# One layer's state recurrence over pairs of time steps: 128 scan steps in place of 256

## The reference

```python
lam_bar = jnp.exp(lam * dt)
b_bar = ((lam_bar - 1.0) / lam)[:, :, None] * b_mat
bu = jnp.einsum('gpc,bsgc->bsgp', b_bar, ug)
# states[t] = lam_bar * states[t-1] + bu[t], for t = 0 .. 255
_, states = lax.associative_scan(_linear_recurrence_combine, (decay, bu), axis=1)
y = jnp.einsum('gcp,bsgp->bsgc', c_mat, states).real
y = y + d_skip * ug
y = jax.nn.gelu(y)
return y * jax.nn.sigmoid(y @ w_glu + b_glu)
```

## Time and profile before

| what | us |
|---|---|
| three runs, median (lowest to highest) | 1106.88 (1104.37 to 1108.78) |
| the profiled execution: its own time | 1107.08 |
| its span in the trace | 1105.4 |
| TensorE busy | 1082.7 (98%) |
| VectorE busy | 617.5 (56%) |
| ScalarE busy | 402.2 (36%) |
| mean granted clock of TensorE | 0.994 of full |

### The profile page before, as it was taken

The page is one execution under the profiler, slowest core; times in us unless marked ns, Lnnn a source line. Parts: engine busy times, 40 slices in busy tenths (PEclk is TensorE's granted clock), DMA queues, the critical chain, the costliest instruction groups (busy, mean ns, idle before and its releaser), DMA issues.

```text
span 1105.4 us, 17516 instructions
## 1 busy us (share of the span) xinstructions
PE 1082.7 (98%) x7004; PEld 801.5 (73%) x7004; DVE 617.5 (56%) x1249; ACT 402.2 (36%) x652; POOL 6.0 (1%) x21
## 2 busy tenths in 40 slices
PE   9999999999999999999999999999999999999996
PEld 6988778998899999999799994444444444444442
DVE  4999997777568888887978762221111111111112
ACT  6522336466355554546676331111111111111112
POOL 2000000000000000000000000000000000000000
PEclk9999999999999999999999989999999999999998
DMA  8544323544245767776544598999999999999994
GB/s 301 172 161 145 102 89 114 172 172 134 76 153 174 231 231 242 240 255 193 186 138 131 215 405 371 426 429 427 427 426 428 428 427 428 427 427 427 427 427 165
DMA packets 44883, 302.62 MB, mean 274 GB/s; under 512 B 5248, under 2 KB 6400, under 8 KB 30976
## 3 DMA queue, kind: packets, MB, share of 16 engines
q1 hardware_dynamic: 41616, 287.59, 67.0%
q10 hardware_dynamic: 3184, 13.87, 3.5%
HBM read 300.39 MB, written 1.05 MB: 273 GB/s over the span
## 4 chain that ended last, share of the span: by engine, by line
PE 91%; DVE 4%; ACT 2%; issue 1%; DMA 1%; SPq 0%; ACTq 0%; DVEq 0%
PE psum L1989 90%; DMA ring<-in_stream 1%; DVE w_low L1143 1%; ACT w_high L653 1%; DVE arena L1143 1%; PE psum L2773 1%; DVE rt L1146 0%; PE psum L2779 0%; DVE x L1143 0%; DVE h L1146 0%; SPq L469 0%; SPq L472 0%; DVE h_low L1143 0%; DVE h_low L1146 0%; DVE arena L1140 0%
## 5 line engine op out<-in xcount | busy, mean ns | idle before, releaser
L1989 PE MATMUL psum<-experts_held,arena 128*64 128x512 f32 x1536 | 333.6, 593 | 2.2 <-DVE scatter_turned L1139 1.0
L1989 PEld LDWEIGHTS psum<-experts_held,arena 128*64 128x64 f32 x1536 | 111.2, 137 | 212.0 <-issue 211.1
L1143 DVE TENSOR_TENSOR w_low<-ring,w_high 128x1024 fp32r<-128x1024 f32 x150 | 180.4, 1219 | 35.7 <-ACT w_high L653 35.0
L653 ACT CAST w_high<-ring 128x1024 fp32r<-128x1024 f32 x150 | 154.5, 1047 | 63.1 <-DMA ring<-in_stream 54.9
L1989 PE MATMUL psum<-h_high,w_high 128*128 128x256 f32 x528 | 133.0, 287 | 3.9 <-ACT arena L736 1.8
L1989 PE MATMUL psum<-h_low,w_high 128*128 128x256 f32 x528 | 131.0, 283 | 0.0
L1989 PE MATMUL psum<-y_high,w_high 128*128 128x256 f32 x480 | 123.1, 285 | 0.5 <-issue 0.3
L1143 DVE TENSOR_TENSOR arena<-arena,psum 128x512 f32<-128x512 f32 (+1 forms) x31 | 19.3, 631 | 182.4 <-ACT arena L1072 181.6
L1989 PE MATMUL psum<-y_low,w_high 128*128 128x256 f32 x480 | 119.6, 283 | 0.0
L1989 PEld LDWEIGHTS psum<-h_high,w_high 128*128 128x128 f32 x528 | 101.2, 192 | 6.2 <-ACT arena L736 2.0
L1989 PEld LDWEIGHTS psum<-h_low,w_high 128*128 128x128 f32 x528 | 101.2, 192 | 0.2
(11 more groups left out here) (269 smaller groups left out, 1262.4 us busy)
## 6 DMA issues: line engine op xcount, KB each, us to landing
experts_held<-in_experts SPq DMA_DIRECT2D x84, 2048.0 KB, 27.2
ring<-in_stream SPq DMA_DIRECT2D x180, 512.0 KB, 3.5
experts_held<-in_experts ACTq DMA_DIRECT2D x12, 1024.0 KB, 7.3
experts_held<-in_experts SPq DMA_DIRECT2D x12, 1024.0 KB, 12.7
x<-in_xT SPq DMA_DIRECT2D x2, 512.0 KB, 7.7
out_y<-experts_held SPq DMA_DIRECT2D x4, 256.0 KB, 3.1
arena<-in_memT SPq DMA_DIRECT2D x1, 512.0 KB, 8.8
bbd<-in_ssm_b SPq DMA_DIRECT2D x1, 512.0 KB, 11.7
```

The costliest lines, as they stand in the source:

```text
L653: act.copy(wh[:, high_slot(m)], ring[:, n_ % RING]).then_inc(hi_ready, 1)
L1143: return dve.tensor_tensor(o, a, b, op)
L1989: return pe.matmul(o, a, b, start=start, stop=stop, skip_group_check=True)
```

## The change

The recurrence over single steps, s[t] = L s[t-1] + b[t], is run over pairs: s[2n+1] = L^2 s[2n-1] + (b[2n+1] + L b[2n]). The scan then has 128 steps.

- `uT` is stored with the even times first and the odd times behind (ScalarE's eviction of `u`). ScalarE makes a second copy `u_in` (8 copies on 32 partitions) in which each state tile has 64 rows, its channels at even and at odd times, with zeros in the rows of the neighbour tile. Two state tiles make a pair j of 0..7.
- The input weights are computed on VectorE (`b_both`: the matrix b, and b times `lam_bar`), transposed by TensorE (16 transposes, in two lots between the `v` units), and evicted by ScalarE (`b_in`, 4 copies). One input matmul then has 128 rows and 256 columns (two tiles of 128 pair steps).
- `recurrence(j)` runs 8 times in place of 16, each on the same 256 columns; it has four scans of 128 steps with the squared decay `rad2` in place of two of 256.
- Outputs at odd times come from the states with `cbd`, `neg`, as before, 128 columns. Outputs at even times t = 2n come from the state at 2n-1 with new matrices `cbd_even`, `neg_even` (the old ones times `lam_bar`; a second call of `output_matrices`), 127 columns, plus the direct part of the input at 2n: a block product `skip`, whose 32x32 blocks TensorE computes once (`skip_weights`, 32 matmuls of 32 columns) and ScalarE puts in place, and which is one 128x128 matmul in each `outputs_of`.
- The rotation table goes over 128 steps, so the last doubling goes away; its first power is the doubled angle.
- VectorE's order of the mixer is rewritten to two recurrences a round; the fillers stay as they are.
- The two halves of a wide expert place share one semaphore; `ssm_b` has 1 MB in place of 512 KB.

```diff
-        rot = view(0, 2, STILES, T)
+        rot = view(0, 2, STILES, STEPS)
+        rot_pairs = view(0, 2, SPAIRS, T)
...
+            for q in range(4):
+                for a in range(2):
+                    at = 64 * (q % 2) + 32 * a
+                    act.copy(u_in[at:at + 32, :, :, q // 2, q % 2],
+                             uT[32 * q:32 * q + 32, :, a * STEPS:a * STEPS + STEPS].rearrange(
+                                 "p (s i) n -> p s i n", s=2)).then_inc(u_ready, 1)
...
+            def turned_inputs(c):
+                act.wait_ge(b_turned, c + 1)
+                for half in range(2):
+                    act.copy(b_in[:, c, 4 * half:4 * half + 4].rearrange("p m n -> p (m n)"), psum[4 + half][:]
+                             ).then_inc(b_ready, 1)
...
+            link(tt_(rad2, rad, rad, ALU.mult))
+            tt_(ptmp[:, 0], fre, lr, ALU.mult)
+            tt_(ptmp[:, 1], fim, li, ALU.mult)
+            tt_(ptmp[:, 2], fre, li, ALU.mult)
+            link(tt_(ptmp[:, 3], fim, lr, ALU.mult))
+            tt_(gre, ptmp[:, 0], ptmp[:, 1], ALU.subtract)
+            link(tt_(gim, ptmp[:, 2], ptmp[:, 3], ALU.add))
 
             weights_low("q", 2)
-            link(dve.tensor_copy(powers[:, 0, 0], cos))
-            link(dve.tensor_copy(powers[:, 0, 1], sin))
+            dve.wait_ge(s_par, 16 * 2)
+            lrb, lib = (v.unsqueeze(2).to_broadcast([P, STILES, 32]) for v in (lr, li))
+            m1, m2 = (v[:, 0:STILES * 32].rearrange("p (j n) -> p j n", j=STILES) for v in (ta, tb))
+            tt_(m1, b_both[:, 0, :, 32:64], lrb, ALU.mult)
+            link(tt_(m2, b_both[:, 1, :, 32:64], lib, ALU.mult))
+            link(tt_(b_both[:, 0, :, 0:32], m1, m2, ALU.subtract))
+            tt_(m1, b_both[:, 0, :, 32:64], lib, ALU.mult)
+            link(tt_(m2, b_both[:, 1, :, 32:64], lrb, ALU.mult))
+            link(tt_(b_both[:, 1, :, 0:32], m1, m2, ALU.add))
+            dve.nop().then_inc(b_scaled, 1)
...
-            while w < T:
+            while w < STEPS:
...
                 for c in range(2):
-                    ins = dve.tensor_tensor_scan(wr[:, c], r_, vr[:, c], 0.0, ALU.mult, ALU.add)
+                    for b in range(2):
+                        some = slice(b * STEPS, b * STEPS + STEPS)
+                        ins = dve.tensor_tensor_scan(wr[:, c, some], rad2[:, 2 * j + b:2 * j + b + 1].to_broadcast([P, STEPS]),
+                                                     vr[:, c, some], 0.0, ALU.mult, ALU.add)
...
             recurrence(0)
+            masked_scores(0)
+            output_matrices(fre, fim, cbd, neg)
             recurrence(1)
-            masked_scores(0)
-            output_matrices()
-            recurrence(2)
-            recurrence(3)
             softplus(0)
+            output_matrices(gre, gim, cbd_even, neg_even)
             for r in range(1, ROUNDS):
-                recurrence(4 * r)
+                recurrence(2 * r)
                 log_weights(r - 1)
                 y_out(r - 1)
-                recurrence(4 * r + 1)
                 masked_scores(r)
-                recurrence(4 * r + 2)
-                if r == ROUNDS - 1:
-                    softplus(r)
-                recurrence(4 * r + 3)
-                if r < ROUNDS - 1:
-                    softplus(r)
+                recurrence(2 * r + 1)
+                softplus(r)
                 values_rest(r - 1)
...
+            split_rows(v_banks, "v", (h0h, h0l), 0, 1)
+            turned_inputs(0)
+            split_rows(v_banks, "v", (h0h, h0l), 1, 3)
+            turned_inputs(1)
+            split_rows(v_banks, "v", (h0h, h0l), 3, 4)
...
             def inputs_of(j):
 
-                i, q = j // 4, j % 4
-                for b in range(2):
-                    hbk.claim(pe, ("bu", j + b))
+                hbk.claim(pe, ("bu", j))
+                bank = hbk.bank(("bu", j))
+                moving = u_in[:, j // 4, j % 4 // 2, j % 2].rearrange("p b n -> p (b n)")
                 for c in range(2):
-                    for b in range(2):
-                        row = slice(32 * (q + b), 32 * (q + b) + 32)
-                        ins = mm(hbk.bank(("bu", j + b))[:, c * T:c * T + T], bbd[row, c, i], uT[row, i], True, True)
-                        if c:
-                            ins.then_inc(bu_done, 1)
+                    ins = mm(bank[:, c * T:c * T + T], b_in[:, c, j], moving, True, True)
+                ins.then_inc(bu_done, 1)
+
+            def skip_weights():
+
+                pe.wait_ge(ssm_ready, 2)
+                for j in range(STILES):
+                    i, q = j // 4, j % 4
+                    for c in range(2):
+                        ins = mm(STAT[32 * q:32 * q + 32, 32 * i:32 * i + 32], b_both[:, c, j, 32:64], cbd[:, c, j], c == 0,
+                                 c == 1)
+                ins.then_inc(skip_done, 1)
...
+                mm(STAT[:, 0:STEPS], skip[:, r], uT[:, r, 0:STEPS], True, False)
+                for even, terms in enumerate((((cbd[:, 0], 0), (neg, 3), (cbd[:, 1], 2), (cbd[:, 1], 1)),
+                                              ((cbd_even[:, 0], 0), (neg_even, 3), (cbd_even[:, 1], 2),
+                                               (cbd_even[:, 1], 1)))):
+                    for n, (matrix, product) in enumerate(terms):
+                        for q in range(4):
+                            made = st[:, (2 * r + q // 2) % 4, product, (q % 2) * STEPS:(q % 2) * STEPS + STEPS - even]
+                            o = STAT[32 * q:32 * q + 32, 1:STEPS] if even else STAT[32 * q:32 * q + 32, STEPS:T]
+                            ins = mm(o, matrix[:, 4 * r + q], made, False, n == 3)
```

151 lines of the change are left out of this document (97 added, 54 removed).

## The result

The changed kernel takes 1112.19 us (median of 6 runs, 1110.73 to 1112.83), the kernel before 1107.12 us in the runs beside it (6 runs, 1104.37 to 1108.78). The ratio is 1.0052, 95% interval 1.0039 to 1.0064: slower by about 5 us. The forecast was 1114.5 us with a range of 1110 to 1120.

The account below looks back on a forecast made before the run. TensorE was taken to set the mixer's pace, VectorE nearly full but just in time. Terms 3.4 + 2.0 + 2.6 + 0.9 - 1.3 = +7.6 us on 1107.08 gave 1114.7, 1114.5 for the median; range 1110 to 1120.

Parts of the forecast that it names:

- A: Weight units q3 and k2: VectorE's new work ahead of q3 makes TensorE stall, +3.4 us.
- B: The `v` units: 16 added transposes of 128x128 on TensorE, in two lots, +2.0 us.
- C: `skip_weights`: 32 matmuls, 64 records at 0.04 us each on TensorE, +2.6 us.
- D: Outputs, four rounds: narrower groups cost nothing extra, the new direct-part matmul adds +0.9 us.
- E: Inputs: full-height matmuls take 0.9 us a call in place of 1.06, eight times, -1.3 us.
- Rival 2: Skip weights and outputs: narrow instructions have a floor, +3.8 and +7 us or one of them; 1118.3 to 1125.3 us; chance 0.12.
- Rival 3: Stall at q3 and k2: smaller than forecast, 1 us or less; time 1112 us or less; chance 0.13.
- Rival 4: Mixer, 71.4 to 182.4 us: VectorE set the pace through unlisted waits; 1107 us or below; chance 0.10.
- Rival 1: Stall at q3: TensorE's idle 2.9 us halves the clock, costing 3.4 us more; time 1117.5 us; chance 0.15.
- Everything behind 190 us moves with TensorE: Behind the mixer: everything, expert weight DMA included, hangs on TensorE's progress, the stretch unchanged in length.

Follow-up runs that it names:

- e1: The changed kernel with VectorE's new work moved behind the weight units' low parts, transposes two units later, one filler before the first inputs; 1108.01 us, ratio 1.0014.
- e2: The kernel before with only VectorE's new work (seven small operations, six products, results unused) put ahead of q3's low part; 1108.93 us, ratio 1.0020.
- e6: The changed kernel with each input matmul reading only 64 of its 128 rows; 1112.42 us, ratio 1.0057 to the kernel before.
- e4: The kernel before with the eight odd-j recurrences leaving out their input products, sums and scans; 1106.68 us, ratio 1.0000.
- e8: The kernel before with six gate units done in two rounded parts, their low parts behind the rotation table's last doublings; 1115.96 us, ratio 1.0092.
- e9: The kernel before with six gate units in two parts, low parts at four places between operations of the last two table doublings; 1110.67 us, ratio 1.0035.
- e3: The kernel before with only the shared semaphore for the two halves of a wide expert place; 1106.43 us, ratio 1.0002.
- e11: The changed kernel with 150 empty instructions ahead of TensorE's program; 1112.68 us, ratio 1.0051 to the kernel before.
- e7: The changed kernel with VectorE's new work moved as in e1 and six gate units done in two rounded parts; 1104.63 us, ratio 0.9983.

## Why the prediction came out right

The mechanism held: TensorE set the pace, VectorE's savings were worth nothing, and its new work ahead of q3 stalled TensorE. By its terms, in us of TensorE's time in the mixer:

| term | predicted | measured | from |
|---|---|---|---|
| A, stall at q3 and k2 | +3.4 | +3.6 | 3.0 and 0.4 from start to start, 0.1 on the records behind each; e1 gives back 3.6, e2 puts 2.7 in |
| B, 16 transposes | +2.0 | +1.8 | two lots of 0.79 and 0.09 on the matmul behind each |
| C, `skip_weights` | +2.6 | +0.9 | 1.74 less 0.87 |
| D, outputs | +0.9 | +0.9 | four times 2.19 less 1.86, less 0.1 each that stood on the filler ahead before |
| E, inputs | -1.3 | -2.0 | about ten changes of shape fewer, 0.2 each |
| sum | +7.6 | +5.2 | mixer's length +5.15 |

The forecast for the time was right to 2.3 us, and the sum for the mixer to 2.4; the difference is two terms of size, C and E, both forecast too dear. That the times differ by the same 5.1 us as the mixers is partly luck: behind the mixer a wait of 1.1 us came in, and half clock at the router took some of it away (below). Term C failed at its price of 0.04 us a record, which was taken between a load of 32 columns (0.027) and the rows of one moving column (0.10): 64 records in 0.87 us are 0.014 each. Even the lower bound was too high, since it took a load's length for a distance between starts. These blocks stand on different rows and columns of the array, and their records, 0.2 us long each, overlap far more than that. Term E failed in that it counted only 0.16 for a call, and even its bound of -1.7 was passed: it priced the inputs by themselves, while a change of shape costs 0.1 us on the record at its other side as well, as e6 shows. Summed over the mixer, the inputs went from 8.48 to 7.43 us (0.10 of the second is left out here, the entry to `skip_weights`), the fillers from 92.04 to 90.77, of which 0.4 belong to D, and the last `v` unit lost 0.09.

Rival 2 (narrow instructions have a floor) is refuted on both halves: 0.014 us a record in `skip_weights` and not 0.10, and a group of four outputs takes half of what a wide one took. The Trainium skill ("TensorE: Matmul & The Clock Gate", section "Wait — 56ns, not 53.3ns?") says that starts are never less than about 25 ns apart, however small the matmuls. By that figure `skip_weights` would have taken 1.6 us, an estimate, where the trace has 0.87; the trace does not agree.

- *Rival 3* (the stall is 1 us or less) is refuted by the timeline: 3.6 us.
- *Rival 4* (VectorE set the pace) is refuted by e4, and by e1, where VectorE's gain stays and the loss is 1.5 us.
- *Rival 1* (the stall halves the clock) did not happen in the profile of the changed kernel (1.00 in [50.4, 53.8]), but did in e2's, where it cost 1.6 us, and at the longer stalls of e8 and e9. The clock falls in some executions and not in others, and the reason that was given against it is wrong: the wait of 1.8 us at 36.9 did not do it in the kernel before, but in four of the twelve profiles it did.
- *"Everything behind 190 us moves with TensorE"* held for 217 to 648 us and failed twice behind it. At the router, 6.8 us at half clock became 3.4, which took 1.7 us off the span; in all twelve profiles this stretch has 0, 3.4 or 6.8 us of it, whatever the kernel, and a profile pair is worth no more than that. At the last expert loads TensorE waits 1.1 us for a DMA, which gives some back.

That last wait is small but regular: 0.9 to 1.5 us in the changed kernel and the four made from it, 0 to 0.6 in the kernel before and the six made from it. In both the load stream runs at 427 GB/s through the whole stage, so the loads hardly lead. The last of the earlier trace rows and its like of after show the DMA share at 1.01 and 1.03. The times at which the 16 DMA engines report each of the last loads show the difference: against TensorE's progress the middle engine is as early in both to 0.3 us, and the slowest one is 1.5 to 1.8 us behind it in the kernel before and those made from it (2.4 in e9), and 2.5 to 2.9 in the changed one and those made from it. A load counts when the slowest has done its share. The shared semaphore doesn't put it back (e3). The code loads do, as far as the traces show: the lag moves in steps, and all 37 steps up of more than 0.25 us between one expert load and the next, in the twelve profiles from 700 us on, stand where a load of 16 KB of code starts (from 2.5 us before the first of the two landings to the second), though only 295 of the 940 pairs have one there. The last such step in the kernel before is from 0.6 to 1.5 us, with the code load of 1064.9; in the changed kernel it is from 1.4 to 2.5, with that of 1057.3. Why some programs end higher than others is open.

Also open is 1 us of bookkeeping: mixer +5.15 and the DMA wait +1.1 make more than the 5.1 us between the medians. The lowest times, 1110.73 and 1104.37 us, are 6.4 apart, which is about the two together, so the missing part is likely half clock, of which the median execution of the kernel before has more. One thing that goes this way is shown in e11: the clock was at 0.50 at 38 us there, TensorE came 1.7 us later to q3, and the stalls shrank to 1.7 us, so its mixer is as long as that of the changed kernel. A loss ahead of a stall is absorbed by it, while in the kernel before it is paid (e3, +1.5 us). How much of the difference of medians that explains wasn't measured.

## What to carry to other kernels

A full bar is not a bound: ask the engine at the end of the chain what it waited for, and if the answer is "nothing", work saved elsewhere is worth zero until something is exchanged for it, as the split units of e7 do. New work on an engine that only just meets its due times belongs behind the last tight one; the same 13 operations cost 3.6 us in front of q3, and behind the tight units no wait. Price matmuls by their changes of shape and their place in the array as well as by their count: going from full to partial height and back cost 0.4 us here, a run of one shape cost nothing extra, and small blocks on different rows and columns run nearly side by side.

## What the runs showed of the hardware

- 64 float32 records of 32x32 in four row and four column places followed each other every 14 ns on average.
- A change of a matmul's shape (128 rows to 64 or 32, and back) cost 0.2 us, 0.1 on the last record ahead of it and 0.1 on the first behind it; within one shape records of 256 columns followed each other every 0.22 us, at 64 rows as at 128. Between full-height matmuls four records of 64 rows, or eight of 32 rows on two places, took 1.06 us, four of 128 rows 0.86.
- A wait of TensorE of 1.8 to 3.6 us was followed by the half clock in some executions and not in others; the stretches were 3.4 or 6.8 us long, and 10.2 in the run with a wait of 8.9 us.
- Over 400 us of full load the slowest of the 16 DMA engines was 0.5 to 2.1 us behind the middle one in the kernel before and 1.3 to 2.9 in the changed kernel; all 37 larger steps up of this lag in the twelve profiles stood at a 16 KB code load.
